# Feed-forward input product of a two-layer trunk: three-pass float32 matmuls against one level of Strassen's recursion, with the weights in a ring of half slots

## The chip, the cores and the metric

The kernel runs on one core of one Trainium2 chip. Its engines are TensorE (PE in the profile, its weight loads are PEld), VectorE (DVE), ScalarE (ACT), GpSimd (POOL) and SyncE (SP), which here only issues loads. Time is device microseconds of one execution, without the host. The kernel before takes 1506.7 us, the median of 3 runs (1506.57 to 1506.76).

## The reference, cut to what matters

The trunk has two layers, over 512 tokens of width 1024. Layer 0 mixes tokens by attention, layer 1 by retention; behind each mixer stands a gated feed-forward block, then a gated embedding. The change is in the feed-forward block's first product.

```
D_MODEL, SEQ, DEPTH, FFN_DIM, CONV_WIDTH = 1024, 512, 2, 2816, 3

def conv_gated_ffn(h, w_in, conv_w, conv_b, w_out):
    s = h.shape[1]
    a = h @ w_in                                    # 512 x 1024 by 1024 x 5632
    gate, up = a[..., :FFN_DIM], a[..., FFN_DIM:]
    gpad = jnp.pad(gate, ((0, 0), (CONV_WIDTH - 1, 0), (0, 0)))
    conv = conv_b + sum(gpad[:, tap:tap + s] * conv_w[tap] for tap in range(CONV_WIDTH))
    return (jax.nn.silu(conv) * up) @ w_out

def reference(x, ...):
    for i in range(DEPTH):
        ...                                         # x = x + mixer
        x = x + conv_gated_ffn(rmsnorm(x, norm_ffn[i]), ffn_w_in[i], ffn_conv_w[i], ffn_conv_b[i], ffn_w_out[i])
        x = per_layer_embed(x, p[i], norm_pl[i], pl_w_gate[i], pl_w_proj[i])
    return rmsnorm(x, norm_final)
```

## The kernel before

Everything is held transposed: 128 features on the partitions, the 512 tokens along the free axis. A product of 128 output features with K input features is K/128 blocks of weights, each 128x128. Float32 is kept by splitting every operand into a high part (rounded to the format fp32r) and a low part (the rest), and by three matmuls for each block (`three`): high by high, high by low, low by high.

Weights come as tiles of 8 blocks (1024 columns, 512 KB) or, for the second product, 11 blocks. SyncE loads a tile into one of two `raw` buffers; ScalarE writes its high part into `wh` (`tile_high`, L1708); GpSimd subtracts, in pieces of 256 columns, and writes the low part into `wl` (`split_low`, L548); TensorE uses both. `wh` and `wl` are rings of four slots.

The feed-forward block has 22 pairs of chunks. A pair f is 128 gate features and the 128 up features that belong to them. In `ffn_in` TensorE makes the gate chunk (8 blocks, 24 matmuls of 512 columns) and then the up chunk, each in a PSUM bank of its own; four banks go round. VectorE takes a gate chunk (L1346, times the norm's 1/rms `rstd`), applies the three taps (L1348, L1352 twice), takes the up chunk (L1355), multiplies (L1358) and makes the low part of the result (L1108); ScalarE gives the silu (L1889) and the high part. The results of all 22 pairs are kept in `yh` and `yl`. After the last pair `ffn_out` makes 8 output chunks, each over 22 blocks, and VectorE adds each to `x`.

Ahead of each feed-forward block stands the mixer's output product, also 8 chunks, which end 5.6 us apart in layer 0 and 2.8 us apart in layer 1. As each chunk ends, VectorE adds it to `x` (L1148), ScalarE writes the high part of the scaled `x` and its square, and VectorE makes the low part (L1128) and adds the square (L1122): this is `x_phase`. The feed-forward product works on `x` before the division by the rms, so it need not wait for the norm: two matmuls (L626, L627) sum the squares over the partitions after the first chunk, and ScalarE turns them into `rstd` by Ln and Exp (L1740, L1742), with a load of an activation table ahead of them and one behind.

Nothing is scheduled by a planner: each engine's instructions stand in the order in which the source gives them, and each engine works through its own in that order. A wait holds back all that stands behind it on its engine.

## Time and profile before

| what | us |
|---|---|
| median of 3 runs | 1506.7 |
| span of the profiled execution, first to last instruction | 1505.3 |
| TensorE busy | 1491.1 |
| VectorE, ScalarE, GpSimd busy | 849.0, 676.1, 795.6 |
| first product of the block, layer 0 (278.3 to 518.3) | 240.0 |
| second product, layer 0 (518.3 to 638.0) | 119.7 |
| first product, layer 1 (1077.7 to 1317.9) | 240.2 |

The profile lists no other time for the execution than its span. The median lies 1.4 us above it, which is what a run has outside its first and last instruction. Starts are in us from the span's start. A matmul's duration includes its way through the array and overlaps the next one, so the pace of matmuls is read from the distance between starts. A row with "x4" is four instructions of one kind in a row, with the time from the first one's start to the last one's end. The granted TensorE clock is 1.00 of full speed through all the stretches of the table.

### The profile page before, as it was taken

How to read it: one execution, taken by the hardware profiler on the slowest of the kernel's cores; microseconds unless marked ns; L12 is line 12 of the kernel's file. 1: busy time of each engine (PE TensorE's matmuls, PEld its weight loads, DVE VectorE, ACT ScalarE, POOL GpSimd, SP SyncE). 2: the span in 40 equal slices, each digit the busy share in tenths (PEclk: the TensorE clock that was granted, in tenths of full speed). 3: DMA queues.
4: the chain of work that ended last, by engine and by line, in shares of the span. 5: the costliest groups of instructions: out<-in, count | busy, mean ns of one | idle time of the engine just before them, and what ended most of it. 6: DMA issues, size and time to landing. Idle time of an engine off the chain costs nothing.

```text
span 1505.3 us, 19989 instructions
## 1 busy us (share of the span) xinstructions
PE 1491.1 (99%) x6808; PEld 1234.9 (82%) x6808; DVE 849.0 (56%) x1294; ACT 676.1 (45%) x1019; POOL 795.6 (53%) x980
## 2 busy tenths in 40 slices
PE   9999999999999999999999999999999999999997
PEld 6888888888888888888888888888788888888886
DVE  7998996455555411159874655646755555511145
ACT  6887886433323322237563543635633333322243
POOL 5343344666666755457345253551566666655452
PEclk9999999999999999999999999999999999999999
DMA  4121111322222322242132322320222222332221
GB/s 178 57 71 56 42 56 63 106 98 98 98 98 98 133 103 97 73 168 99 56 143 102 107 89 85 133 99 33 94 104 91 98 97 98 118 111 97 93 80 60
DMA packets 42838, 142.14 MB, mean 94 GB/s; under 512 B 4256, under 2 KB 10528, under 8 KB 42784
## 3 DMA queue, kind: packets, MB, share of 16 engines
q1 hardware_dynamic: 41248, 138.82, 26.3%
q10 hardware_dynamic: 1536, 2.61, 0.5%
q8 instruction: 32, 0.52, 0.1%
q14 instruction: 22, 0.18, 0.0%
HBM read 139.32 MB, written 2.10 MB: 94 GB/s over the span
## 4 chain that ended last, share of the span: by engine, by line
PE 96%; DVE 2%; ACT 1%; DMA 1%; issue 0%; POOL 0%; SPq 0%; POOLq 0%; DVEq 0%; ACTq 0%
PE bank L602 26%; PE bank L605 26%; PE bank L606 26%; PE bank L880 3%; PE bank L885 3%; PE bank L884 3%; PE bank L680 2%; PE bank L660 1%; PE bank L661 1%; PE bank L691 1%; PE bank L690 1%; DMA x<-in_xT 1%; PE bank L1033 0%; DVE sumsq L1122 0%; PE bank L663 0%
## 5 line engine op out<-in xcount | busy, mean ns | idle before, releaser
L548 POOL TENSOR_TENSOR wl<-raw,wh 128x256 fp32r<-128x256 f32 x752 | 616.1, 852 | 476.4 <-ACT wh L1708 476.4
L602 PE MATMUL bank<-xh,wh 128*128 128x512 f32 (+1 forms) x1160 | 451.4, 389 | 1.0 <-DVE xl L1128 0.8
L606 PE MATMUL bank<-xh,wl 128*128 128x512 f32 (+1 forms) x1160 | 450.2, 388 | 0.0
L1708 ACT ACTIVATE wh<-raw 128x1024 fp32r<-128x1024 f32 (+1 forms) x212 | 235.0, 1108 | 478.8 <-PE bank L602 388.7
L605 PE MATMUL bank<-xl,wh 128*128 128x512 f32 (+1 forms) x1160 | 450.0, 388 | 0.0
L602 PEld LDWEIGHTS bank<-xh,wh 128*128 128x128 f32 x1160 | 217.8, 188 | 47.2 <-DVE xl L1128 2.1
L606 PEld LDWEIGHTS bank<-xh,wl 128*128 128x128 f32 x1160 | 217.9, 188 | 44.7
L605 PEld LDWEIGHTS bank<-xl,wh 128*128 128x128 f32 x1160 | 217.8, 188 | 43.8
L564 POOL TENSOR_TENSOR wl<-raw,wh 128x256 fp32r<-128x256 f32 x160 | 127.2, 827 | 194.4 <-ACT wh L1708 194.4
L1148 DVE TENSOR_TENSOR x<-x,bank 128x512 f32<-128x512 f32 x56 | 38.5, 688 | 254.0 <-PE bank L606 254.0
L602 PE MATMUL bank<-yh,wh 128*128 128x512 f32 x352 | 136.9, 389 | 0.0
L605 PE MATMUL bank<-yl,wh 128*128 128x512 f32 x352 | 136.9, 389 | 0.0
L606 PE MATMUL bank<-yh,wl 128*128 128x512 f32 x352 | 136.9, 389 | 0.0
L1352 DVE SCALAR_TENSOR_TENSOR conv<-gate,par,conv 128x512 f32<-128x512 f32 x88 | 91.8, 1043 | 13.2 <-DVE conv L1348 5.0
L1346 DVE TENSOR_TENSOR gate<-bank,rstd 128x512 f32<-128x512 f32 x44 | 30.4, 692 | 91.8 <-PE bank L606 87.0
L606 PEld LDWEIGHTS bank<-yh,wl 128*128 128x128 f32 x352 | 66.1, 188 | 13.8
L602 PEld LDWEIGHTS bank<-yh,wh 128*128 128x128 f32 x352 | 66.1, 188 | 13.8
L605 PEld LDWEIGHTS bank<-yl,wh 128*128 128x128 f32 x352 | 66.1, 188 | 13.5
L1889 ACT ACTIVATE conv<-conv 128x512 f32<-128x512 f32 x44 | 27.9, 634 | 105.8 <-DVE conv L1352 105.8
L1355 DVE TENSOR_TENSOR up<-bank,rstd 128x512 f32<-128x512 f32 x44 | 30.4, 692 | 68.1 <-PE bank L606 68.1
L1108 DVE TENSOR_TENSOR yl<-yf,yh 128x512 f32 x44 | 41.6, 946 | 40.1 <-ACT yh L1708 40.1
L880 PE MATMUL bank<-wh,sums_h 128*128 128x512 f32 x128 | 50.8, 397 | 0.2 <-ACT sg L1968 0.2
(224 smaller groups left out, 2332.4 us busy)
## 6 DMA issues: line engine op xcount, KB each, us to landing
raw<-in_w SPq DMA_DIRECT2D x180, 512.0 KB, 3.2
raw<-in_w SPq DMA_DIRECT2D x32, 704.0 KB, 4.0
rc<-in_w SPq DMA_DIRECT2D x16, 512.0 KB, 3.8
w_end<-in_w SPq DMA_DIRECT2D x8, 512.0 KB, 4.1
rb<-in_w SPq DMA_DIRECT2D x8, 512.0 KB, 5.9
x<-in_xT SPq DMA_DIRECT2D x4, 512.0 KB, 7.5
pin<-in_pT ACTq DMA_DIRECT2D x2, 512.0 KB, 3.1
rotary<-in_consts ACTq DMA_DIRECT2D x1, 512.0 KB, 3.5
```

Source lines behind the costliest of these rows:

```text
L548: last = nc.gpsimd.tensor_tensor(wl[:, slot, cols], part[:, cols], wh[:, slot, cols].bitcast(F32), ALU.subtract)
L564: last = nc.gpsimd.tensor_tensor(wl[:, slot_of(n), cols], part[:, cols] if len(part.shape) == 2 else part[:, b, :], wh[:, slot_of(n), cols ...
L602: first = mm(out, ah_, bh_, start=start, stop=False, skip_group_check=True)
L605: mm(out, ah_, bl_, start=False, stop=False, skip_group_check=True)
L606: return mm(out, al_, bh_, start=False, stop=stop, skip_group_check=True)
L880: first = mm(out[:], high, wh[:, slot, cols], start=start and k == 0, stop=False, skip_group_check=True)
L884: mm(out[:], high, wl[:, slot, cols], start=False, stop=False, skip_group_check=True)
L885: last = mm(out[:], low_, wh[:, slot, cols], start=False, stop=k == KC // 2 - 1, skip_group_check=True)
L1108: vec.tensor_tensor(out, full, high.bitcast(F32), ALU.subtract).then_inc(done, 1)
L1148: vec.tensor_tensor(one(x, k), one(x, k), bank[u][:], ALU.add).then_inc(chunk_freed, 1)
L1352: vec.scalar_tensor_tensor(cv, g[:, tap:tap + T], col(par, w[tap]), cv, ALU.mult, ALU.add).then_inc(conv_step, 1)
L1708: nc.scalar.activation(out, in_, ACT.Copy, bias=0.0, scale=scale).then_inc(done, 1)
```

## The change

Let A be the weights of a pair, X the input; the K axis is cut in halves, the tokens are cut in an early and a late half of 256, and the two chunks of a pair (gate and up) are the halves of the output. Each is then a 2x2 block problem, and one level of Strassen's recursion (in Winograd's form) gives it by 7 half-size products instead of 8:

* 7 products for each pair, each 4 blocks and 12 matmuls of 256 columns, of these weights: A11, A12, A22 as they are, and S1, S2, S3, S4, which are sums. VectorE makes the sums for each pair: S1 and S3 by one instruction of 1024 elements (`sums_31`, out of `raw` with A21 broadcast), S2 and S4 by one of 512 each.
* The input's sums T1 to T4 (half the K axis by half the tokens) are made once in each layer, together with their high and low parts, at the end of `x_phase` and behind it.
* The weights' ring has 11 half slots of 512 columns. Each of the 7 pieces gets a high part by ScalarE (`piece_high`, 512 columns) and a low part: GpSimd makes six (two instructions of 256 columns each, `piece_lows`), VectorE the one of S4.
* A pair is loaded at once, 1024 KB, into one of two halves of `raw`. The half is free for the next but one load when S4 is summed and GpSimd has made the low part of A22.
* Three products of a pair pile up in one bank: ScalarE copies it (256 columns) after each of A11, S2 and S3 ("snapshots"), before TensorE may add the next. VectorE adds the snapshots to the other banks: `late_up`, `gate_sum`; `late_up_scaled`, `early_up`, `gate_scaled` multiply by `rstd`. The convolution's last tap goes to ScalarE (`tap`), the other two stay on VectorE and work in PSUM.
* The pairs are done in two phases of 11. After each phase the 8 output chunks are made over the 11 blocks of the phase and added to `x`, so `yh` and `yl` hold 11 pairs.

TensorE's order in the middle of a phase is, in the function `ffn`: A11 of pair f, A22 of f-1, S1 of f, S4 of f-1, S2 of f, A12 of f, S3 of f. The diff, cut to its core:

```diff
+HS = K2 * P
+RING_HS = 11
+PHASES = 2
+def ffn_order():
+    order = []
+    for ph in range(PHASES):
+        a, b, last = ph * FH, ph * FH + 1, ph * FH + FH - 1
+        order += [("A11", a), ("S1", a), ("A12", a), ("A11", b), ("S1", b), ("A12", b), ("S2", a), ("S2", b),
+                  ("S3", a), ("S3", b), ("A22", a), ("S4", a)]
+        for f in range(a + 2, last + 1):
+            order += [("A11", f), ("A22", f - 1), ("S1", f), ("S4", f - 1), ("S2", f), ("A12", f), ("S3", f)]
+        ...
+ON_VECTOR = ("S4",)
...
@@ SyncE: a load of a pair waits for the pair before the last
+                def consumed(item):
+                    kind, t = item
+                    if kind == "P":
+                        sp_eng.wait_ge(f_sum4, pair_no(layer, t) + 1)
+                        sp_eng.wait_ge(f_low_p, low_count(layer, PIECE["A22", t]))
...
@@ GpSimd
+            def piece_lows(layer):
+                for q, (kind, _) in enumerate(PIECES):
+                    if kind in ON_VECTOR:
+                        continue
+                    part, at = piece_source(q), piece_at(layer, q)
+                    blocks_ = FH if kind == "O" else K2
+                    pool.wait_ge(f_high, piece_count(layer, q))
+                    for b in range(0, blocks_, LOW_BLOCKS):
+                        ...
+                        last = nc.gpsimd.tensor_tensor(wl[:, held], part[:, cols], wh[:, held].bitcast(F32),
+                                                       ALU.subtract)
+                    last.then_inc(f_low_p, 1)
...
@@ TensorE
-            def ffn_in(layer, norm):
-                ...
-                        x_blocks(slot_of(n0 + u), bank[u][:], range(KC), norm if first and u == 0 else None)\
-                            .then_inc(chunk_done, 1)
-                        if first and u == 0:
-                            stats(norm)
+                def product(kind, f, out, start, stop):
+                    q = PIECE[kind, f]
+                    low_ready(q)
+                    for k in range(K2):
+                        last = three(out, *weights(q, k), *operands[kind](k), start and k == 0, stop and k == K2 - 1,
+                                     begins=k == 0, begun=f_begun)
+                    last.then_inc(f_prod, 1)
+                ...
+                def p2(f, ph):
+                    if f == 0:
+                        pe.wait_ge(x_low, KC * norm + KC)
+                ...
+                def p6(f):
+                    pe.wait_ge(f_snap1, pair_no(layer, f) + 1)
+                    ...
+                    product("S2", f, pair_banks(f)[0], False, False)
+                def p7(f):
+                    pe.wait_ge(f_snap2, pair_no(layer, f) + 1)
+                    ...
+                    product("S3", f, pair_banks(f)[0], False, False)
+                def p4(f):
+                    pe.wait_ge(f_snap3, pair_no(layer, f) + 1)
+                    ...
+                    product("A22", f, pair_banks(f)[0], False, True)
+                ...
+                    for f in range(a + 2, end + 1):
+                        p1(f, ph)
+                        p4(f - 1)
+                        p5(f, ph)
+                        p3(f - 1)
+                        p6(f)
+                        p2(f, ph)
+                        p7(f)
...
@@ VectorE
+            def sums_31(layer, f):
+                ...
+                dve.wait_ge(f_loaded[region], count)
+                others = raw_blocks(("P", f)).rearrange("p (a c) -> p a c", c=HS)[:, 0:4:3, :]
+                vec.tensor_tensor(s31[:, f % 2, :, :], others,
+                                  quarter(f, "A21").unsqueeze(1).to_broadcast([P, 2, HS]), ALU.add).then_inc(f_sum31, 1)
...
@@ ScalarE
+            def snapshot(layer, f, kind, j, done):
+                act.wait_ge(f_prod, product_count(layer, kind, f))
+                copy(snap[:, f % 2, j, :], pair_banks(f)[0], done)
```

How the instructions stand on the engines shows at three places. The first is VectorE in the middle of the first product. Before, one pair is (from its gate chunk on; `ISA` and `REGISTER_ALU` rows are the sequencer's):

```order
L1346 TENSOR_TENSOR gate<-bank,rstd 128x512 [waits chunk_done]
L1348 ISA [waits chunk_freed]
L1348 TENSOR_SCALAR conv<-gate,par 128x512
...
L1352 SCALAR_TENSOR_TENSOR conv<-gate,par,conv 128x512
...
L1352 SCALAR_TENSOR_TENSOR conv<-gate,par,conv 128x512
...
L1355 TENSOR_TENSOR up<-bank,rstd 128x512 [waits chunk_done]
...
L1358 TENSOR_TENSOR yf<-conv,up 128x512 [waits gate_silu]
L1108 ISA [waits y_high]
L1108 TENSOR_TENSOR yl<-yf,yh 128x512
```

Now one turn of the loop is these 13, of which `s<-` are the sums for the pair after the next, `wl<-s,wh` is S4's low part, and `wide_bank` is PSUM:

```order
L1714 TENSOR_TENSOR up<-wide_bank,snap 128x256 [waits f_snap3]
L1718 SCALAR_TENSOR_TENSOR up<-up,rstd 128x256 [waits f_up2]
L1751 TENSOR_TENSOR wide_bank<-wide_bank,up 128x512 [waits gate_silu,f_up1,f_up]
L1510 TENSOR_TENSOR s<-raw 128x1024 [waits f_loaded1,f_low_p]
L1377 TENSOR_TENSOR yl<-wide_bank,yh 128x512 [waits y_high]
L1724 SCALAR_TENSOR_TENSOR up<-wide_bank,rstd 128x256 [waits f_prod]
L1518 TENSOR_TENSOR s<-s,raw 128x512 [waits f_sum31,f_sum4,f_low_p]
L1377 TENSOR_TENSOR wl<-s,wh 128x512 [waits f_high]
L1732 TENSOR_TENSOR wide_bank<-wide_bank,snap 128x2x256 [waits f_prod]
L1736 TENSOR_TENSOR gate<-wide_bank,rstd 128x512 [waits f_gsum]
L1524 TENSOR_TENSOR s<-s,raw 128x512 [waits f_sum2,f_low_v]
L1742 SCALAR_TENSOR_TENSOR wide_bank<-gate,par,wide_bank 128x512 [waits conv_tap]
```

The thirteenth is a second row of L1742's kind (L1744). Seven instructions for a pair have become thirteen, five of which read two operands in SBUF: L1718, L1510, L1518, the second L1377 and L1524.

The second place is ScalarE in the same loop, one turn, from the third snapshot of pair f-1 on:

```order
L2148 ACTIVATE snap<-wide_bank 128x256 [waits f_prod]
L2148 ACTIVATE wh<-raw 128x512 [waits f_loaded0,f_begun]
L2431 ACTIVATE wide_bank<-wide_bank 128x512 [waits conv_step]
L2148 ACTIVATE snap<-wide_bank 128x256 [waits f_prod,f_gsum]
L2148 ACTIVATE wh<-raw 128x512 [waits f_loaded1,f_begun]
L2148 ACTIVATE yh<-wide_bank 128x512 [waits y_full]
L2148 ACTIVATE wh<-s 128x512 [waits f_sum31,f_begun]
L2148 ACTIVATE wh<-s 128x512 [waits f_sum4,f_begun]
L2148 ACTIVATE wh<-s 128x512 [waits f_sum2,f_begun]
L2148 ACTIVATE snap<-wide_bank 128x256 [waits f_prod]
L2426 ACTIVATE wide_bank<-gate,par 128x512 [waits y_low,f_gate]
L2148 ACTIVATE wh<-raw 128x512 [waits f_loaded0,f_begun]
```

One more `wh<-s` (S3) ends the turn. The second row is A11 of pair f+1, the first to need that pair's load; silu, the snapshots and the high part of y stand behind it. Before, a turn was two casts of 1024 columns, one silu and one high part.

The third place is ScalarE at the start of the block, behind the last chunk of `x_phase` (`t`, `xg` and `th` hold the input's sums):

```order
L2148 ACTIVATE th<-t 128x1024 [waits t2_made]
L2148 ACTIVATE wh<-s 128x512 [waits f_sum31,f_begun]
L2148 ACTIVATE th<-xg 128x1024 [waits t3_made]
L2148 ACTIVATE snap<-wide_bank 128x256 [waits f_prod]
L2148 ACTIVATE wh<-raw 128x512 [waits f_loaded0,f_begun]
L2148 ACTIVATE th<-t 128x1024 [waits t4_made]
L2447 ACT_TABLE_LOAD
L2148 ACTIVATE wh<-s 128x512 [waits f_sum4,f_begun]
L2148 ACTIVATE snap<-wide_bank 128x256 [waits f_prod] x3
L2230 ACTIVATE ln_ms<-wide_bank,eps 128x512 [waits stat_done]
L2232 ACTIVATE rstd<-ln_ms 128x512 [waits ms_ln]
L2463 ACT_TABLE_LOAD
```

Before, only the table loads, Ln and Exp stood there. Now the first snapshot stands behind the high part of T3, and the next three behind that of T4.

## Rows read from the trace of the kernel before

**Rows 1.** Page, part 1: busy us of each engine, share of the span, instructions.
```profile
PE 1491.1 (99%) x6808; PEld 1234.9 (82%) x6808; DVE 849.0 (56%) x1294; ACT 676.1 (45%) x1019; POOL 795.6 (53%) x980
```
**Rows 2.** Busy time by stretch: length, PE, PEld, DVE, ACT, POOL, TensorE clock.
```profile
278.30:518.30 240.00, 240.00 (x1060) 198.49 (x1059) 127.26 (x159) 79.90 (x93) 157.01 (x181) 1.00 0.28 100
```
**Rows 3.** Timeline of TensorE, embedding's last chunk: start, us, operation.
```profile
1479.84 0.39 PE L602 MATMUL bank<-xh,wh 128*128 128x512 f32 x1
...
1487.09 0.39 PE L606 MATMUL bank<-xh,wl 128*128 128x512 f32 x1
1487.32 0.28 PE L602 MATMUL bank<-xh,wh 128*128 128x256 f32 x1
...
1492.95 0.28 PE L606 MATMUL bank<-xh,wl 128*128 128x256 f32 x1
```
**Rows 4.** Timeline of GpSimd and VectorE, three tiles' low parts.
```profile
652.20 2.83 POOL L548 TENSOR_TENSOR wl<-raw,wh 128x256 fp32r<-128x256 f32 x4 [4.24 <-ACT wh L1708]
...
481.85 3.74 POOL L548 TENSOR_TENSOR wl<-raw,wh 128x256 fp32r<-128x256 f32 x4 [2.24 <-ACT wh L1708]
481.99 1.15 DVE L1352 SCALAR_TENSOR_TENSOR conv<-gate,par,conv 128x512 f32<-128x512 f32 x1 [0.15 <-DVE conv L1348]
483.29 0.99 DVE L1352 SCALAR_TENSOR_TENSOR conv<-gate,par,conv 128x512 f32<-128x512 f32 x1 [0.15 <-DVE conv L1352]
...
487.20 3.28 POOL L548 TENSOR_TENSOR wl<-raw,wh 128x256 fp32r<-128x256 f32 x4 [1.61 <-ACT wh L1708]
488.26 0.93 DVE L1108 TENSOR_TENSOR yl<-yf,yh 128x512 f32 x1 [0.92 <-ACT yh L1708]
```
**Rows 5.** The same in retention, with a VectorE instruction of 1024 elements.
```profile
918.88 2.42 POOL L564 TENSOR_TENSOR wl<-raw,wh 128x256 fp32r<-128x256 f32 x2
919.22 1.49 DVE L1440 TENSOR_TENSOR w_end<-rc,w_end 128x1024 f32<-128x1024 f32 x1
```
**Rows 6.** Groups of VectorE, whole span: count, busy us, mean ns, idle before.
```profile
L1108 DVE TENSOR_TENSOR al<-sp,ah 128x256 fp32r<-128x256 f32 x16 | 6.7, 419 | 2.3 <-ACT ah L1708 2.2
L1108 DVE TENSOR_TENSOR wl<-ahead,wh 128x1024 fp32r<-128x1024 f32 x2 | 2.4, 1212 | 0.0
```
**Rows 7.** Groups of ScalarE, whole span.
```profile
L1708 ACT ACTIVATE pinh<-pin 128x512 fp32r<-128x512 f32 x4 | 2.3, 624 | 8.8 <-DMA pin<-in_pT 8.8
L1829 ACT ACTIVATE sp<-bank 128x256 f32<-128x256 f32 x16 | 6.1, 382 | 1.1
L1708 ACT ACTIVATE sums_h<-sums 128x1024 fp32r<-128x1024 f32 x4 | 4.2, 1052 | 0.0
L2042 ACT ACT_TABLE_LOAD x4 | 5.1, 1283 | 0.1
```
**Rows 8.** Loads: count, KB each, median us from issue to landing.
```profile
raw<-in_w SPq DMA_DIRECT2D x180, 512.0 KB, 3.2
raw<-in_w SPq DMA_DIRECT2D x32, 704.0 KB, 4.0
```
**Rows 9.** Timeline of VectorE and ScalarE at the first product's start, layer 0.
```profile
272.87 0.69 DVE L1148 TENSOR_TENSOR x<-x,bank 128x512 f32<-128x512 f32 x1 [3.48 <-PE bank L606]
...
278.47 0.69 DVE L1148 TENSOR_TENSOR x<-x,bank 128x512 f32<-128x512 f32 x1 [3.65 <-PE bank L606]
279.08 0.75 DVE L1128 SCALAR_TENSOR_TENSOR xl<-x,par,xh 128x512 fp32r<-128x512 f32 x1
279.74 0.68 DVE L1122 TENSOR_TENSOR sumsq<-sumsq,bank 128x512 f32<-128x512 f32 x1
...
284.51 0.69 ACT L1740 ACTIVATE ln_ms<-bank,eps 128x512 f32<-128x512 f32 x1 [1.76 <-PE bank L627]
285.23 0.63 ACT L1742 ACTIVATE rstd<-ln_ms 128x512 f32<-128x512 f32 x1
```
**Rows 10.** Timeline of VectorE there in layer 1: the last two chunks.
```profile
1075.09 0.69 DVE L1148 TENSOR_TENSOR x<-x,bank 128x512 f32<-128x512 f32 x1 [0.85 <-PE bank L606]
...
1077.89 0.69 DVE L1148 TENSOR_TENSOR x<-x,bank 128x512 f32<-128x512 f32 x1 [0.26 <-PE bank L606]
```

More of the change, by code:

```diff
@@ L58 @@
 FFN_IN_TILES, FFN_OUT_TILES = 2 * FC, 2 * KC
+K2 = KC // 2
 PL_TILES = KC * PC // W8 + KC
@@ new lines, with done_by, ffn_ring @@
+OUT_AT = (6, 0, 3, 6, 0, 3, 8, 5)
+def done_by(q):
+    kind, t = PIECES[q]
+    if kind == "O" and t % KC < 2:
+        return PIECE["O", t - t % KC + 2]
+    return q + 1
+def ffn_ring(layer):
+    at, free, held, p = [], [], {}, RING_FROM[layer]
+    for q, (kind, t) in enumerate(PIECES):
+        p = OUT_AT[t % KC] if kind == "O" else (p + (q in RING_SKIPS[layer])) % RING_HS
+        slots = range(p, p + (3 if kind == "O" else 1))
+        at.append(p)
+        free.append(max(done_by(held[i]) + 1 if i in held else 0 for i in slots))
+        assert free[-1] <= q and slots[-1] < RING_HS
+        held.update((i, q) for i in slots)
+        p = slots[-1] + 1
+    return at, free, held
@@ L131, with item_load @@
+def item_load(layer, item):
+    i = ITEM[item]
+    return i % 2, 16 * (layer * len(ITEMS) // 2 + i // 2 + 1)
 C_COS, C_SIN, C_DECAY = 0, T, 2 * T
@@ new lines, in x_phase @@
+                    if k == K2 + 3:
+                        sum_2(layer, 1)
+                t2(2)
+                t2(3)
+                x_low_part(norm, KC - 1)
+                add_square(norm, KC - 1, (KC - 1) % 2)
+                sum_high(norm)
+                negative_lows(1, 1)
+                sum_low(norm)
+                for k in range(K2):
+                    t3(k)
+                t3_lows()
+                for k in range(K2):
+                    t4(k)
+                negative_lows(2, 3)
@@ L1471, in tile_low @@
                 dve.wait_ge(w_high, casts(n))
-                low(pieces(wl[:, slot_of(n), cols], part), part, pieces(wh[:, slot_of(n), cols], part), done)
+                held = slot_cols(slot_of(n), cols)
+                low(pieces(wl[:, held], part), part, pieces(wh[:, held], part), done)
             def rotate_first(h, which):
@@ L1719, in tile_high @@
                     act.wait_ge(ready, count)
-                    copy(pieces(wh[:, slot, 0:W8 * P], part), part, w_high)
+                    copy(pieces(wh[:, slot_cols(slot, slice(0, W8 * P))], part), part, w_high)
                     return
+                for layer in range(2):
+                    if N_PL[layer] <= like < N_PL[layer] + RING:
+                        ffn_left(layer, slot)
+                        free = 0
                 if free:
```

736 lines of the change are left out of this document (561 added, 175 removed).

## Prediction, written before the changed kernel was run

> **What bounds the kernel now.** I read the page's busy times first: TensorE works 1491.1 of 1505.3 us and no other engine over 56% [rows 1]. So time falls only where TensorE gets less to do or its pace changes, and an engine beside it matters once it is slower than TensorE for the same work. The stretch of the changed product shows the room: of 240.0 us GpSimd is busy 157.0, VectorE 127.3, ScalarE 79.9, at a full granted clock [rows 2]. For one of the 22 pairs that is 10.9 us of TensorE with 7.1 of GpSimd and 5.8 of VectorE beside it. Then I read the pace of matmuls from their starts, where embedding's last chunk goes from full to half size. 512 columns: 33 steps from 1479.84 to 1487.32, 0.2267 us each. 256 columns: 47 steps from 1487.32 to 1492.95, 0.120 each [rows 3]. Last I read what GpSimd and VectorE do to each other [rows 4, 5], because the change loads just these two.
>
> **TensorE's part.** A pair was 48 matmuls x 0.2267 = 10.88 us and becomes 84 x 0.120 = 10.08: 0.80 us less, 44 pairs, **-35.2 us**. That is the whole gain; an eighth less arithmetic would be 1.36 us a pair, but a half-size matmul takes 53% of a full one.
>
> The Trainium skill (TensorE: Matmul & The Clock Gate, Back-to-back issue gap) gives a warm gap of N/2.4 + 2.5 ns. By it a pair would go from 10.36 to 9.17 us and the gain would be 52 us. The rows have 48 half-size matmuls in a row at 0.120, so they decide.
>
> The second product keeps its 3 x 11 x 16 matmuls; cut in two halves it costs VectorE 8 more additions of 0.69 us in each layer, beside chunks of 7.5 us: nothing.
>
> **GpSimd's part.** Four instructions of 256 columns alone take 2.83 us, one is 0.74 long, so they start 0.70 apart [rows 4]. With one VectorE instruction of 512 elements that reads two operands in SBUF the four take 3.28, with two 3.74: +0.45 each. With one of 1024 elements, two take 2.42 instead of 0.70 + 0.74 = 1.44: +0.98 [rows 5]. The new turn asks 6 pieces x 2 = 12 instructions, 8.4 us, and VectorE has five such instructions in it: three of 512 (1.34), one of 1024 (0.98), one of 256 (no row; between 0 and 0.45, I take 0.18: half of the step from 512 to 1024, 0.27, below the 0.45). Sum **10.9 us a pair**, against 10.08 of TensorE. Before it was 3.74 + 3.28 = 7.0 against 10.9.
>
> **VectorE's part.** One turn is three instructions of 256 (0.42 each), nine of 512 (0.69) and one of 1024 (1.21): 8.7 us [rows 6, 9]. Neighbours overlap by 0.08 (0.69 long, 0.61 from start to start, rows 9), nine times: -0.7. Three wait for the one before them, 0.15 each [rows 4]: +0.45. The five with two SBUF operands wait for GpSimd's instruction to end: 0.93, 0.99 and 1.15 instead of 0.69 [rows 4], +0.24 to +0.46 each, so +1.2 to +2.3. Together 9.7 to 10.8, I take 10.1: level with TensorE. It is a ring with ScalarE: third snapshot, VectorE down to `gate_scaled` (7.7), tap, two casts, next snapshot (0.63 + 2 x 0.62 + 0.38 with 0.1 for each hand-over), also some 10.1 us, and each turn TensorE's A22 waits for that snapshot. ScalarE alone has 7 casts x 0.62, 3 x 0.38 and three of 0.62: 7.3 us [rows 7], room enough.
>
> **Can a lead hide GpSimd's 10.9?** It could if GpSimd could start a phase far ahead. It can't for long: the load of pair f+2 waits for the low part of A22 of pair f. 512 KB land after 3.2 us and 704 after 4.0 [rows 8]; going on at that slope, 1024 KB take 5.3. Behind the load stands ScalarE's cast of A11 of f+2, and behind that silu, the next snapshot and, through silu, VectorE's whole turn. By the durations above GpSimd ends A22 some 3.8 us after it starts A11, so ScalarE's next A11 is free 9.1 us after GpSimd's last A11 began; ScalarE is there after 10.1. Each turn GpSimd falls 0.8 behind; within one or two turns the load comes later than ScalarE, and from there every turn lasts what GpSimd's lasts. 9 of the 11 pairs of a phase stand in this loop, 36 in all: 36 x (10.86 - 10.08) = **+28 us**, less some 3 for the first turns: **+25**.
>
> **The start of each block.** Count from VectorE's addition of the last chunk (278.47 in layer 0; TensorE goes on at 278.27) [rows 9]. Before, the first product wanted the last low part of `x` after 7/8 of 5.4 us. Now A12, third in line, wants it after 2.9. VectorE has six instructions up to it (two of 0.75, four shorter): ready at 4.0. Then come the squares, the high and low parts of T2 and of the squares, four T3 of 0.34, with GpSimd's port delays: 9.7. ScalarE's high part of T3 (1.05), VectorE's low part (1.21), four T4 (1.4), ScalarE's high part of T4 (1.05), a table load (1.28), the cast of S4 (0.62) and only then the snapshot (0.38) that the second pair's S2 waits for: 17.2 with hand-overs [rows 7]. TensorE has seven products before it, 10.1 us, and stands there 7.4 us. Ln, Exp and a table load (0.69 + 0.63 + 1.28) ahead of the first S3 snapshot cost 0.5 more. Last, in the first turn of the loop ScalarE's third snapshot stands behind the tap, which needs S4's product, two VectorE instructions and itself: 4.1 us after that product, where TensorE has one product of 1.44 to do: 2.7. Together **+10.6** in layer 0. In layer 1 chunks end 2.8 us apart instead of 5.6 [rows 10], while VectorE now has some 15 us of work from the fifth chunk on in 8.4 us; it comes 3.2 later: **+13.8**. The second phase of each block has only the last of these stalls, its casts done beside the second product: 2 x 2.7 = **+5.4**. Without port delays the first two would be 8 and 11; if DMA landings or the bank waits come late, some 4 more each.
>
> **Sum.** -35.2 + 25 + 10.6 + 13.8 + 5.4 = +19.6 us. The sum is against the profiled span, 1505.3, which becomes 1525; the 1.4 us around it stay, so the forecast is **1526 us** against the median of 1506.7.
>
> **Rivals.**
> *TensorE's pace holds (GpSimd is not the bound).* If five VectorE instructions don't all meet a busy GpSimd, its turn is nearer 8.4 + 1.2 = 9.6 and VectorE's 9.7. Then loops run at 10.1 and the 25 becomes 1: 1502; with starts at their lower bound, 1494. For it: in this stretch before, VectorE's instructions met GpSimd by their place in the turn, and other places may miss it. Against it: a GpSimd busy for over 9 of 10 us leaves no place to miss. Chance 0.18.
> *The two engines hold each other up more than summed.* Each VectorE instruction waits 0.46 and GpSimd idles for casts that ScalarE has late in its turn (A12 and S3 stand last): 11.5 us a turn, 36 x 0.64 = 23 more than forecast: 1549. For it: three rings lie within 0.8 us of each other, and what one loses another rarely gives back. Chance 0.12.
> *The port is held for a whole instruction.* Then five instructions, 0.42 + 1.21 + 3 x 0.69 = 3.7 us, go fully on GpSimd's 8.4: 12.1 a pair, 1526 + 36 x 1.2 = 1569. Against it: +0.45 for 0.69 in three places [rows 4]. Chance 0.02. [...]
> *The starts overlap far better than I chain them*, half of the 30 us, with the loop as forecast: 1511. Inside the forecast's own range.
>
> **Chances.** The forecast with its own range (1508 to 1540) has 0.68. Within 0.2% (3 us, about what this kernel's runs can tell from no change, 1503.7 to 1509.7) lies the upper edge of the first rival and the lower edge of the forecast: 0.08. Faster by more: most of the first rival, 0.16. Slower by more: 0.76. The range for 8 in 10 takes in the first rival's upper half and the second rival: 1497 to 1549.
>
> **What would show it.** In the changed kernel's profile: matmuls of 256 columns 0.120 apart inside a product, and a turn of the loop (A11 of one pair to A11 of the next) of 10.9 instead of 10.1 us; TensorE idle ahead of A22's first matmul, put down to ScalarE's snapshot; GpSimd busy 9 tenths or more through a phase, its instructions at 0.74 and 1.19 us; 5 us loads that ScalarE's A11 cast waits for. At the start of each block one idle of some 7 us ahead of the second S2 and one of 2 to 3 ahead of the first A22 in the loop. A loop at 10.1 us proves the GpSimd step wrong; 11 us with GpSimd idle for a fifth of it proves the bound to be a ring of waits and not its work; a granted clock below 1.00 in the phases would be a cost I have at nothing.

## The result, and the profile after

| | before | after |
|---|---|---|
| median, us | 1506.7 | 1587.9 (1586.2 to 1590.3, 4 runs) |
| ratio | | 1.054 (95% interval 1.0525 to 1.0555) |
| profiled span, us | 1505.3 | 1587.0 |
| two feed-forward blocks, first matmul to first of embedding, us | 359.7 + 359.9 | 395.6 + 404.8 |

The change costs 81 us and the forecast was 1526 (1497 to 1549): right in sign, 62 us short. All of the 81 us lies in the two blocks. The page of the changed kernel, part 1, beside [rows 1]:

```profile
PE 1491.6 (94%) x8392; PEld 1304.4 (82%) x8392; DVE 1062.5 (67%) x1614; ACT 832.2 (52%) x1431; POOL 974.5 (61%) x1156
```
TensorE is idle for 95 us instead of 14, and as busy as before although its matmuls are 35 us less: some of them now run at half the clock (below). Its waits over the span (us in total, times, longest us):

```profile
PE wide_bank L770 <- ACT snap L2148: 43.4, 44, 5.1
PE wide_bank L770 <- POOL wl L719: 14.0, 4, 3.5
PE wide_bank L770 <- DVE xl L1397: 11.5, 4, 8.4
PE wide_bank L770 <- DVE up L1714: 7.9, 2, 4.1
PE wide_bank L770 <- POOL wl L704: 5.1, 2, 4.5
```
The first and third rows I had forecast. The second, fourth and fifth I had not: the second is ahead of the second chunk of the second product in all four phases, the fourth at the start of the two second phases, the fifth once at the start of embedding in layer 1. Busy time by stretch (length, PE, PEld, DVE, ACT, POOL, granted clock), beside [rows 2]: the first phase of layer 0, the second product behind it, the first phase of layer 1, and 68 us inside the loop:

```profile
277.60:411.60 134.00, 116.23 (x904) 113.04 (x903) 109.63 (x150) 76.32 (x140) 114.71 (x128) 0.95 0.23 77
411.60:479.70 68.10, 64.61 (x289) 53.47 (x289) 16.16 (x23) 16.79 (x20) 33.71 (x49) 0.97 0.31 106
1113.10:1253.10 140.00, 117.33 (x904) 114.25 (x903) 115.58 (x156) 78.85 (x145) 121.91 (x135) 0.94 0.22 74
...
334.00:402.00 68.00, 63.78 (x520) 62.50 (x519) 58.31 (x79) 41.10 (x81) 66.95 (x75) 1.00 0.30 103
```
In the loop GpSimd is busy 66.95 of 68.00. The timeline of TensorE there: A11's first matmuls of three pairs in a row, and the waits between the first two (start, us, operation, idle before and releaser):

```profile
334.36 0.28 PE L770 MATMUL wide_bank<-xh,wh 128*128 128x256 f32 x1
...
337.24 0.28 PE L770 MATMUL wide_bank<-xh,wh 128*128 128x256 f32 x1
337.36 0.28 PE L773 MATMUL wide_bank<-xl,wh 128*128 128x256 f32 x1
...
341.56 0.28 PE L770 MATMUL wide_bank<-xh,wh 128*128 128x256 f32 x1
...
344.28 0.39 PE L770 MATMUL wide_bank<-th,wh 128*128 128x256 f32 x1 [1.12 <-ACT snap L2148]
...
345.82 0.28 PE L770 MATMUL wide_bank<-xh,wh 128*128 128x256 f32 x1
...
356.64 0.28 PE L770 MATMUL wide_bank<-xh,wh 128*128 128x256 f32 x1
```
Half-size matmuls start 0.120 apart, as in [rows 3], and two turns last 11.46 and 10.82. I laid the two blocks out by such starts of products. A stretch's excess over the pace is its length less its matmuls at 0.120 and 0.2267. A phase's loop is counted here from the A11 of its fourth pair to the first matmul of the second product, which is 8 turns; what lies ahead of that A11 is the start:

| | forecast | measured, us |
|---|---|---|
| pace, 44 pairs | -35.2 | -35.2 |
| loop, turns of 10.86 forecast, 10.98 measured (mean of 32) | +25 | +28.8 |
| start of each phase, up to the fourth pair's A11, over the pace | +29.8 | +61.8 (18.5, 8.8, 25.0, 9.5) |
| second product, four stretches over 62.8 | 0 | +26.6 (5.4, 6.5, 3.8, 11.0) |

The sum, +82, is the 81 us within the 1 us of statistics matmuls that stand in the starts. Two rows of the forecast held and two did not.

### The profile page after: what moved, and what is told of

It is laid out like the page before. It is cut to its first block, busy times and chain, and to the rows that moved or that the text cites. A ratio compares the mean times of both kernels' runs of the same rounds, so it can differ in the third digit from the quotient of the medians.

```text
span 1587.0 us, 23224 instructions
## 1 busy us (share of the span) xinstructions
PE 1491.6 (94%) x8392; PEld 1304.4 (82%) x8392; DVE 1062.5 (67%) x1614; ACT 832.2 (52%) x1431; POOL 974.5 (61%) x1156
## 4 chain that ended last, share of the span: by engine, by line
PE 63%; POOL 16%; DVE 8%; DMA 6%; ACT 4%; issue 3%; SPq 0%; DVEq 0%; ACTq 0%; POOLq 0%
PE wide_bank L770 16%; PE wide_bank L774 16%; PE wide_bank L773 16%; POOL wl L719 15%; DMA raw<-in_w 5%; PE wide_bank L1151 3%; PE wide_bank L1156 3%; PE wide_bank L1155 3%; PE wide_bank L849 2%; ACT wh L2148 2%; DVE s L1510 2%; DVE wl L1377 1%; DVE s L1518 1%; DVE gate L1736 1%; DVE wide_bank L1732 1%
## 5 line engine op out<-in xcount | busy, mean ns | idle before, releaser
L2148 ACT ACTIVATE wh<-raw 128x512 fp32r<-128x512 f32 (+2 forms) x264 | 230.8, 877 | 341.8 <-PE wide_bank L770 130.5
L770 PE MATMUL wide_bank<-xh,wh 128*128 128x256 f32 (+1 forms) x1160 | 380.6, 328 | 20.4 <-DVE xl L1397 11.5
L773 PE MATMUL wide_bank<-xl,wh 128*128 128x256 f32 (+1 forms) x1160 | 378.3, 326 | 0.0
L774 PE MATMUL wide_bank<-xh,wl 128*128 128x256 f32 (+1 forms) x1160 | 378.2, 326 | 0.0
L770 PEld LDWEIGHTS wide_bank<-xh,wh 128*128 128x128 f32 x1160 | 224.2, 193 | 40.0 <-DVE xl L1397 13.2
L719 POOL TENSOR_TENSOR wl<-s,wh 128x256 fp32r<-128x256 f32 x264 | 237.9, 927 | 6.4 <-ACT wh L2148 6.4
L774 PEld LDWEIGHTS wide_bank<-xh,wl 128*128 128x128 f32 x1160 | 223.8, 193 | 17.6
L773 PEld LDWEIGHTS wide_bank<-xl,wh 128*128 128x128 f32 x1160 | 224.2, 193 | 16.3
L770 PE MATMUL wide_bank<-th,wh 128*128 128x256 f32 x528 | 158.1, 299 | 43.4 <-ACT snap L2148 43.4
L774 PE MATMUL wide_bank<-th,wl 128*128 128x256 f32 x528 | 152.7, 289 | 0.0
```

What stands on the lines that cost most here:

```text
L719: last = nc.gpsimd.tensor_tensor(wl[:, held], part[:, cols], wh[:, held].bitcast(F32), ALU.subtract)
L770: first = mm(out, ah_, bh_, start=start, stop=False, skip_group_check=True)
L773: mm(out, ah_, bl_, start=False, stop=False, skip_group_check=True)
L774: return mm(out, al_, bh_, start=False, stop=stop, skip_group_check=True)
L2148: nc.scalar.activation(out, in_, ACT.Copy, bias=0.0, scale=scale).then_inc(done, 1)
```

## Experiments

All times are medians; "before" ran beside each at 1506.8 to 1506.9. e4, e6 and e12 ran once, the others four times. A turn is the mean of the 32 turns from the fourth pair's A11 of each phase on, "starts" the third row of the table above.

| kernel | us | ratio to before (95%) | turn | starts |
|---|---|---|---|---|
| after | 1587.9 | 1.054 (1.0525 to 1.0555) | 10.98 | 61.8 |
| e1 O1's cast first | 1566.0 | 1.0391 (1.0374 to 1.0409) | 10.88 | 62.5 |
| e2 ScalarE's start order | 1580.2 | 1.0489 (1.0472 to 1.0507) | 10.91 | 54.9 |
| e4 two lows less | 1563.7 (one run) | | 10.16 | 61.1 |
| e5 filled waits | 1585.8 | 1.052 (1.0503 to 1.0538) | 11.00 | 58.5 |
| e6 = e1 + up2 in PSUM | 1561.5 (one run) | | 10.78 | 60.6 |
| e7 = e6 + S2's low shared | 1557.3 | 1.033 (1.0312 to 1.0349) | 10.67 | 62.2 |
| e8 = e1 + up2 first | 1568.5 | 1.0413 (1.0394 to 1.0432) | 10.88 | 64.8 |
| e9 = e8 + start orders | 1558.7 | 1.0347 (1.0328 to 1.0365) | 10.89 | 53.9 |
| e10 = e7 + casts first | 1541.2 | 1.0229 (1.0212 to 1.0246) | 10.25 | 58.3 |
| e11 = e10 + start orders | 1535.1 | 1.0187 (1.017 to 1.0204) | 10.27 | 51.2 |
| e12 = e11, parts of T3 and T4 left out | 1535.5 (one run) | | 10.34 | 48.8 |
| e13 = e11 + snapshots first | 1535.5 | 1.0192 (1.0175 to 1.0209) | 10.27 | 51.7 |

### e1: the second product's wait

```diff
+                        if f == end + 1:
+                            high("O", KC * ph + 1)
                         if f <= end + 1:
                             tap(f - 1)
...
-                        if f > end:
+                        if f > end + 1:
```


> One edit: ScalarE's cast of the second output slot's weights (O1) stands ahead of the last pair's tap instead of behind it. Theory (order in ScalarE's queue): in the changed kernel TensorE waits 3.5 us four times ahead of the second chunk of the second product, because that cast (1.37) and GpSimd's six lows (3.9) start only after the tap, at 419.55 in the first phase, while the weights' transfer should have landed some 4 us earlier. With the edit the wait goes in all four phases: 14 us, and with it some of the 7.6 us that these stretches lose at a granted clock of 0.5: 1566 to 1574 us. Rival (the slot or the transfer is late, not the cast): the cast starts at the same time as before, and the time stays at 1587 to 1589.

ScalarE, GpSimd and TensorE of the changed kernel there:

```profile
413.70 0.60 ACT L2148 ACTIVATE yh<-wide_bank 128x512 fp32r<-128x512 f32 x1 [1.07 <-DVE wide_bank L1751]
418.83 0.78 ACT L2426 ACTIVATE wide_bank<-gate,par 128x512 f32<-128x512 f32 x1 [4.54 <-DVE gate L1736]
419.55 1.37 ACT L2148 ACTIVATE wh<-raw 128x1408 fp32r<-128x1408 f32 x1
...
421.00 4.58 POOL L719 TENSOR_TENSOR wl<-raw,wh 128x256 fp32r<-128x256 f32 x7 [9.77 <-ACT wh L2148]
...
424.93 0.63 PE L770 MATMUL wide_bank<-yh,wh 128*128 128x512 f32 x1 [3.49 <-POOL wl L719]
```
and ScalarE in e1:

```profile
413.77 1.38 ACT L2148 ACTIVATE wh<-raw 128x1408 fp32r<-128x1408 f32 x1 [1.06 <-DMA raw<-in_w]
417.26 0.78 ACT L2426 ACTIVATE wide_bank<-gate,par 128x512 f32<-128x512 f32 x1 [2.10 <-DVE gate L1736]
```
ScalarE and GpSimd stood idle for 4.5 and 9.8 us with the cast queued behind a tap that needs the last S4 product. In e1 the cast waits for the transfer alone, the wait is gone in all four phases, three of the four second products last 62.8 us, and the kernel gains 21.9. That is the theory: 14.0 of waits and, with them, the time at half clock, 7.6 us in the expectation and 6.9 by the stretches below. The fourth second product keeps 4.7 us, from another wait (see "Why the prediction was wrong").

### e4, e6, e7, e10: what bounds the loop

e4: GpSimd's loop over a piece ends after the first half where `kind in ('A12', 'S3')`, from the fourth pair on.

> From the fourth pair of each phase on GpSimd makes only the first half of the low parts of A12 and S3; the second halves are left out (the product uses old values there), nothing else is changed. A turn of the loop has 10 GpSimd instructions instead of 12. Theory (GpSimd's own work is the bound of the loop): 10.98 us a turn less 2 x 0.70 is 9.6, below TensorE's 10.08, so turns fall to TensorE's pace or to VectorE's ring, 10.1 to 10.3, in 28 turns: 19 to 25 us less, 1563 to 1569, and GpSimd shows idle time. Rival (the ring of snapshots, VectorE's turn and the tap holds the loop at 10.98): turns stay over 10.7 with GpSimd idle for over 1 us in each, and the time stays over 1580.

e6 (here f_up2's sum; the multiplication that follows reads the same bank):

```diff
-vec.tensor_tensor(up2[:, f % 2, :], pair_banks(f)[2], ...
+vec.tensor_tensor(bank[6 + f % 2][:, 0:HALF], pair_banks(f)[2], ...
```


> On top of e1 (1566.0 us, loop turns of 10.9): VectorE's sum up2 goes to a free PSUM bank instead of SBUF, so the 256-element multiplication by rstd that follows reads one operand in SBUF instead of two. VectorE's work stays, and one of its five instructions that hold GpSimd up goes. Theory (GpSimd's turn is its 8.4 us plus the holds, and I had no row for this one: 0.18 taken between 0 and 0.45): turns fall by 0.1 to 0.25, 36 turns, 4 to 9 us: 1557 to 1562. Rival (a short instruction holds up nothing): turns and time stay within 0.05 us and 2 us.

e7:

```diff
+            def half_low(layer, f):
+                ...
+                low(wl[:, at:at + HS // 2], s2[:, HS // 2:HS], wh[:, at:at + HS // 2], f_low_x)
...
                         if f < end:
+                            half_low(layer, f + 1)
                             sum_4(layer, f + 1)
```


> On top of e6: from the third pair of each phase on VectorE makes the second half (256 elements) of the low part of S2, so GpSimd has 11 instructions a turn instead of 12 and VectorE one of 0.42 more, which again reads two operands in SBUF. Theory (GpSimd's turn is a sum): less 0.70, plus a hold of 0.1 to 0.25 as in e6, so turns of 10.3 to 10.5 instead of e6's 10.75; 36 x 0.45 is 16 us less than e6: 1542 to 1547. Rival (VectorE's ring is the next bound right away, since it is 0.86 busy and gets work): turns stay over 10.6, gain under 6 us, and GpSimd shows over 0.3 us of idle time a turn.

e10:

```diff
-                        if f <= end + 1:
-                            tap(f - 1)
                         if f < end:
                             high("A12", f + 1)
                             high("S3", f + 1)
+                        if f <= end + 1:
+                            tap(f - 1)
```


> On top of e7 (1557.3 us, turns of 10.67 with GpSimd idle for a tenth): ScalarE casts A12 and S3 of the next pair ahead of the tap instead of behind it. Theory (with GpSimd's share smaller the loop is bound by the ring third snapshot, VectorE down to the gate, tap, two casts, next snapshot, the one that the prediction had at 10.1): the two casts, 1.24 us, leave the ring, turns fall to 10.1 to 10.35, 32 turns: 10 to 18 us less, 1540 to 1547. Rival (VectorE's own work with its waits for GpSimd's port is the bound, no ring): turns stay over 10.6 and the gain is under 3 us.

Busy time in 34 us of the loop for e6, e7 and e10 in this order, and in 68 us for e4 (one fence for each):

```profile
364.00:398.00 34.00, 32.64 (x268) 32.03 (x267) 29.19 (x42) 21.09 (x41) 34.00 (x38) 1.00 0.33 111
```
```profile
364.00:398.00 34.00, 31.15 (x253) 30.34 (x252) 31.48 (x46) 21.18 (x41) 29.93 (x34) 1.00 0.26 93
```
```profile
364.00:398.00 34.00, 34.00 (x280) 33.49 (x280) 33.65 (x48) 22.80 (x42) 34.00 (x38) 1.00 0.29 103
```
```profile
334.00:402.00 68.00, 68.00 (x569) 68.00 (x568) 63.02 (x88) 45.58 (x89) 64.61 (x70) 1.00 0.26 90
```
e4 decides the first question. With two GpSimd instructions less seven of the eight turns of each phase are 10.08, TensorE's pace, and GpSimd still works 64.61 of 68: 9.58 a turn, which is 10.98 less twice 0.70. So in the changed kernel GpSimd's own work is the bound, and the ring of snapshots, with its casts where they were, lets 10.08 through. The turns gave 26.1 us and the kernel's one run is 24.2 below the median; the changed kernel's own four runs differ by 4.

e6 prices the hold that I had no row for: the settled turns in the first phase of layer 0 are 10.96 to 10.99 in e1 and 10.78 to 10.80 in e6, **0.18 us** for an instruction of 0.42, the value I took. The other phases are less even, and over all 32 turns the mean falls by 0.10. The Trainium skill (SBUF — State Buffer, Who interferes with whom) calls the shared port an exclusive lock and says that a VectorE instruction with two SBUF inputs contends with a GpSimd one that reads SBUF. The runs agree on who interferes; the price is less than half of the instruction.

e7 is the miss that taught most. GpSimd lost an instruction and was idle (29.93 of 34 us busy), yet turns fell only to 10.67, 3.6 us over 32 of them (the kernels' times differ by 4.2, and e7's own runs by 4.5). That is the rival's number: a ring of waits. The trace's chain of work in e7 shows which one (start, us, what):

```profile
368.03 0.62 ACT wh L2168
368.72 7.52 POOL wl L728 x8
376.30 4.92 DMA raw<-in_w
381.84 0.59 ACT wide_bank L2451
388.18 0.70 DVE gate L1755
389.63 1.14 ACT wh L2168 x2
```
The cast of A12, eight low parts up to A22's, the load that waits for these, silu (behind the A11 cast that waits for the load), VectorE's work down to the gate, the tap, and the cast of A12 again: 21.6 us for two turns, 10.8 for one. This ring goes through the load and not from snapshot to snapshot as the forecast's. e10 cuts it: the casts of A12 and S3 no longer wait for the tap. Turns are 10.27 to 10.30 with few exceptions, GpSimd and VectorE are both busy for 33.65 us and more of 34, and the kernel gains 16.1 (theory: 10 to 18). The theory's time came true, but its ring isn't shown: taking the two casts out of a ring of snapshots would help as well, and e4 had passed that ring at 10.08 with the casts in it. e10 ran only on top of e7. What its order is worth with all twelve instructions on GpSimd, which are 10.98 a turn by themselves, was not tested.

### e2, e9, e11, e12, e13: the start of a block

e2 moves snapshots, Ln, Exp and table loads ahead on ScalarE:

```diff
                 piece_high(layer, 9)
+                snap1(layer, 0)
+                snap1(layer, 1)
+                nc.scalar.preload_act_table_set("natural_log_exp_and_others")
                 t3_highs(layer)
-                snap1(layer, 0)
+                snap2(layer, 0)
                 piece_high(layer, 10)
+                snap2(layer, 1)
+                norm_scale(norm, FFN_STAT)
+                nc.scalar.preload_act_table(ACT.Silu)
                 t4_highs(layer)
-                nc.scalar.preload_act_table_set("natural_log_exp_and_others")
...
```


> One edit, ScalarE's order at the start of a block: the snapshots of the first two A11 products stand ahead of the high part of T3, those of the two S2 products, Ln, Exp and both table loads ahead of the high part of T4. Theory (snapshots are queued behind work that waits for VectorE): the two waits ahead of the S2 products (2.4 and 3.9 in layer 0, 0.9 and 5.1 in layer 1) go, about 2 us come back ahead of A22, which needs T4, so A22 of the first pair starts some 7 us earlier in each layer; with the clock that falls in these waits 12 to 20 us in all: 1568 to 1576. Rival (VectorE and GpSimd set the start whatever ScalarE's order is): the second pair's A22 waits as much longer as the S2 waits shrink, and the time stays within 4 us of 1588.

e9 has this, e8, and on VectorE:

```diff
                     if k == K2 + 1:
                         t1_lows()
                         sum_2(layer, 0)
-                        sums_31(layer, 1)
                     if k == K2 + 2:
                         t2(0)
                         t2(1)
-                        sum_4(layer, 0)
-                    if k == K2 + 3:
-                        sum_2(layer, 1)
+                x_low_part(norm, KC - 1)
+                sums_31(layer, 1)
                 t2(2)
                 t2(3)
-                x_low_part(norm, KC - 1)
                 add_square(norm, KC - 1, (KC - 1) % 2)
+                sum_4(layer, 0)
+                negative_lows(1, 1)
+                sum_2(layer, 1)
                 sum_high(norm)
-                negative_lows(1, 1)
...
```


> On top of e8: ScalarE's start order of e2, and VectorE's at the start of a block: the low part of the last chunk of x directly behind its addition, the sums S3 and S1 of the second pair, S4 of the first and S2 of the second behind it instead of ahead of it (ScalarE's casts follow). Theory (the waits at the start are VectorE's queue: in layer 1 it does 5.6 us of sums ahead of the last chunk's low part, and TensorE waits 8.4 us for that): the wait ahead of the first A12 falls to under 1.5 in layer 0 and to 2 to 4 in layer 1, and the first A22 starts 8 to 12 us earlier than in e1 in layer 0 and 10 to 14 in layer 1: 1535 to 1548. Rival (VectorE's sum of work in the start is the bound, wherever the sums stand): the wait ahead of A12 goes but A22 starts no more than 7 us earlier, as with ScalarE's order alone: 1550 to 1556.

> On top of e10: the orders of VectorE and ScalarE at the start of a block from e9, without e8's edit. Theory (the loops and the starts are separate costs, so gains add): e9 took 8.6 us off the starts of e1 (62.5 to 53.9 over the pace of 10.08); the same comes off e10: 1531 to 1540, still slower than before's 1506.9. Rival (the earlier start only moves the wait into the first turns of the loop, where GpSimd has not got ahead): less than 3 us off e10.

VectorE of the changed kernel in layer 1 around the last addition of a chunk, and the TensorE wait behind it, answering [rows 10]:

```profile
1111.41 1.22 DVE L1518 TENSOR_TENSOR s<-s,raw 128x512 f32<-128x512 f32 x1
1112.56 1.75 DVE L1510 TENSOR_TENSOR s<-raw 128x1024 f32<-128x1024 f32 x1
1114.24 0.68 DVE L1417 TENSOR_TENSOR x<-x,wide_bank 128x512 f32<-128x512 f32 x1
...
1118.50 1.21 DVE L1524 TENSOR_TENSOR s<-s,raw 128x512 f32<-128x512 f32 x1
1119.63 0.67 DVE L1417 TENSOR_TENSOR x<-x,wide_bank 128x512 f32<-128x512 f32 x1
...
1125.03 0.58 PE L770 MATMUL wide_bank<-xh,wh 128*128 128x256 f32 x1 [8.36 <-DVE xl L1397]
```
The last chunk's addition comes 6.5 us after TensorE went on (1113.1), not 3.2 as I had it, in part since sums of 0.69 and 1.21 take 1.2 and 1.75 beside a busy GpSimd. e9 takes the wait to 3.4 in layer 1 and to nothing in layer 0, as its theory had it. But the first A22, counted from the block's first matmul, comes only 4.5 and 7.1 us earlier than in e1, the rival's bound, and the kernel takes 1558.7, 9.8 less than e8, 7.4 less than e1, and over both expected ranges (1535 to 1548, the rival's 1550 to 1556). ScalarE's order alone (e2) gave 7.7, where its theory had 12 to 20 and its rival at most 4: A22 came 6.2 us earlier in layer 0, and 5.6 in layer 1, but it now waits 2.25 itself in both, the S4 behind it 1.2 and 1.9, and the second pair's A22 still 1.1 and 3.2 (2.9 and 3.4 in the changed kernel). In e11 the start orders give 6.1 without e8, inside the theory's time.

> On top of e11, VectorE makes one of the four instructions for T3 and one of the four for T4 and leaves out the other six (the products that use T3 and T4 then take partly old values); everything else is issued as before. Theory (the start of a block is VectorE's work end to end, with its waits for GpSimd): six instructions of 0.47 to 0.96 us less on its chain, so the first A22 of each block starts 3 to 5 us earlier and the time falls by 6 to 10 us. Rival (ScalarE's queue or the transfers of the next weights set it): under 2 us a block.

> On top of e11 (1535.1 us, computed in full): at the start of a block ScalarE takes the snapshots of the first two A11 products before the casts of S2, S3 and S3 (it waited for VectorE's S2 sum, which waits for GpSimd), and VectorE splits the sum of squares before it makes that S2 sum. Theory (the start is a chain through all three engines, GpSimd's low of S2, VectorE's S2 sum, ScalarE's casts, GpSimd's lows): the wait ahead of the first S2 goes (2.6 us in layer 0, 2.4 in layer 1), but the second S2 and the first A22 hang on the same chain, so A22 starts only about 1 us earlier in each block: 1531 to 1535. Rival (the snapshot is what holds the start, as ScalarE's order in e2 suggested): A22 starts 2.5 us earlier or more in each block: 1528 to 1531.

Both came out as no gain (1535.5 and 1535.5 against 1535.1). In e12 the starts are 2.4 us shorter and the loops 2.2 longer; the first A22 comes no earlier. ScalarE there shows why:

```profile
295.75 0.38 ACT L2165 ACTIVATE snap<-wide_bank 128x256 f32<-128x256 f32 x1 [1.24 <-PE wide_bank L783]
296.21 0.69 ACT L2247 ACTIVATE ln_ms<-wide_bank,eps 128x512 f32<-128x512 f32 x1
296.93 0.63 ACT L2249 ACTIVATE rstd<-ln_ms 128x512 f32<-128x512 f32 x1
297.58 1.28 ACT L2467 ACT_TABLE_LOAD   x1
298.87 1.06 ACT L2165 ACTIVATE th<-t 128x1024 fp32r<-128x1024 f32 x1
```
VectorE had T4 ready at 296.1, but its high part stands behind Ln, Exp and the table load, as my e2 ordered them: the rival of e12. In e13 the first S2 starts 2.2 us earlier in layer 0 and the first A22 at 300.64 instead of 300.72; counted from the block's first matmul it is 0.3 earlier in layer 1. Which order is the shortest for this start stays open: each of the three tried met the next queue.

### e8: the start of the second phase

```diff
-                        if f == a + 1:
-                            sums_31(layer, f + 1)
                         if f <= end + 1:
                             late_up(f - 1)
                             late_up_scaled(f - 1)
+                        if f == a + 1:
+                            sums_31(layer, f + 1)
```


> On top of e1: at the start of each phase VectorE makes the sum up2 of the first pair before it waits for the weights of the third pair (sums S3 and S1), not behind that wait. Theory (VectorE's queue order holds TensorE: at the start of the second phase it stands 7.2 us waiting for a transfer of 4.9 us with up2 queued behind, and TensorE waits 4.0 for up2): the wait ahead of the first S4 goes, but the third pair's A11 needs the same transfer, so some 2 us of it come back there; 2 to 4 us less in each second phase, 0 to 2 in each first: 1557 to 1562. Rival (all of it comes back at the third pair's A11, since the transfer is the bound): the time stays within 2 us of 1566.

The first row is what VectorE waits for between 470 and 500 us in the changed kernel, the second fence is e8's chain of work and TensorE's row:

```profile
DVE s L1510 <- DMA raw<-in_w: 8.7, 2, 7.0
```
```profile
487.47 4.81 DMA raw<-in_w
...
495.50 0.55 PE L770 MATMUL wide_bank<-xh,wh 128*128 128x256 f32 x1 [3.81 <-POOL wl L719]
```
The rival is right that nothing is gained, and the kernel is even 2.4 us slower than e1, just outside its 2 us. In the second phases the wait moves from up2 to the third pair's A11: that pair's 1024 KB can only be asked for when GpSimd has made A22's low part of the phase's first pair, at 487.4, and everything behind it is 4.8 us away. A third place for raw weights would test it directly; that was not tried. The second phases' starts are 0.4 and 0.1 us shorter than in e1, the first phases' 1.5 and 1.4 longer: the loss is there, where the sums of the third pair now stand behind an up2 that waits for its snapshot (in layer 0 they start at 306.6 instead of 303.5).

### e5: what the fallen clock costs

```diff
+                def keep_on(count, at):
+                    for _ in range(count):
+                        mm(bank[at][:, 0:HALF], ones_r[:], xh[:, 0, 0:HALF], start=True, stop=True, ...)
```


> TensorE gets matmuls of 256 columns that nobody reads (into a free bank) where it waits at the start of a block: 16 and 56 ahead of A12 of the first pair (layer 0, layer 1), 14 and 4 ahead of the first S2, 24 and 34 ahead of the second, 16 and 20 ahead of A22 of the second pair, each about two thirds of the wait. No wait is taken away. Theory (the granted clock falls because TensorE stands idle there): the stretches at 0.5 that follow these waits go, and with them most of the 10.5 us that the first phases of the two blocks lose by the clock (4.7 and 5.8): 1576 to 1581 us, granted clock at 1.00 from 290 to 320 and from 1120 to 1170. Rival (the clock falls for another reason, or what follows waits for VectorE anyway): the half-clock stretches stay, or go without the time getting shorter by over 3 us.

The start of the two blocks in the changed kernel, then in e5:

```profile
277.00:330.00 53.00, 39.97 (x282) 38.13 (x281) 40.62 (x56) 27.64 (x48) 35.12 (x39) 0.87 0.17 60
1113.00:1175.00 62.00, 43.97 (x311) 42.61 (x310) 50.07 (x66) 32.05 (x56) 45.12 (x49) 0.86 0.16 52
```
```profile
277.00:330.00 53.00, 46.63 (x371) 44.90 (x371) 40.86 (x57) 28.13 (x49) 38.01 (x42) 1.00 0.17 60
1113.00:1175.00 62.00, 55.41 (x435) 53.63 (x433) 50.11 (x68) 33.81 (x59) 47.05 (x51) 0.97 0.19 67
```
The clock is back and the time falls by only 2.1 us, which is inside the 3 us that the rival allows and within what the changed kernel's runs differ by. The trace says where the rest went. Up to the fourth pair's A11 the two blocks win 2.6 and 2.5 us, over half of the 9 that the stretches at 0.5 had cost there; so a part was hidden behind the other engines' chain and a part was not. The loops behind them then take 0.2 and 0.8 longer, and the second phase of layer 0, which has no filler, starts 1.7 slower in this execution.

## Why the prediction was wrong

**TensorE's part: right.** 0.120 a matmul, -35.2.

**GpSimd's part and "Can a lead hide": right in cause and size.** Turns of 10.98 for 10.86, GpSimd busy 66.95 of 68, loads of 4.9 us for 5.3, and e4's 10.08 with 9.58 of work; the loops cost 28.8 for 25. (The text's own terms, 8.4 + 1.34 + 0.98 + 0.18, give 10.90; it went on with 10.86, 1.4 us less in 36 turns. The first rival's lower end, 1494, is 1497 by the bounds that the text gives for the starts.) The holds of 0.45, 0.98 and 0.18 made the difference to the first rival, and the third rival's whole-instruction price (12.1) is excluded.

**VectorE's ring "some 10.1": not contradicted, but not the next bound.** In e4, with VectorE's and ScalarE's instructions unchanged, turns are 10.08, so the ring takes no more than that there. The text followed the load only as a lag behind GpSimd; what it didn't price is the ring through the load, 10.8 a turn in e7, where VectorE has one instruction more. It cost nothing here, hidden behind GpSimd's 10.98, and it is why taking work off GpSimd alone gave so little.

**"The second product keeps its matmuls ... nothing": the step that failed first.** It counted VectorE's eight more additions and did not follow the new order of casts: O1's cast stands behind a tap that needs the product two before it. 26.6 us for 0; e1 gives back 21.9. The other 4.7 are nearly all a wait of 4.5 for the first tile of embedding in layer 1: its cast waits for TensorE, as I read it for the slot that the last chunk of weights holds. No run changed this:

```profile
1513.40 1.06 ACT L2148 ACTIVATE wh<-raw 128x1024 fp32r<-128x1024 f32 x1 [9.50 <-PE wide_bank L774]
...
1517.87 0.80 PE L770 MATMUL wide_bank<-pinh,wh 128*128 128x512 f32 x1 [4.51 <-POOL wl L704]
```
The text said that such a thing exists ("DMA landings or the bank waits come late, some 4 more each") and put it only at the starts.

**"The start of each block": places right, sizes half.** Layer 0 cost 18.5 for 10.6. The second S2 starts 20.9 us after the block's first matmul, 10.9 over its pace for 7.4: VectorE's chain is longer, with T3's and T4's first two instructions at 0.95 each instead of the 0.47 of their last two. A22 in the first turn waits 2.9 for 2.7. What I left out is the next load, in the chain of work:

```profile
310.01 5.75 DMA raw<-in_w
```
The third pair's 1024 KB are asked for only after the first A22's low part, and from that pair's A11 to the fourth's it takes 15.1 us. Layer 1 cost 25.0 for 13.8, some 3.3 of it since VectorE was 6.5 late and not 3.2.

**The second phases "have only the last of these stalls": wrong.** 8.8 and 9.5 for 2.7. The same load: VectorE waits 7.0 for it with up2 behind (e8). My own sentence on the loop, that a load waits for A22's low part, was not carried to the first turn of a phase, where nothing leads.

**The clock "at nothing": wrong in the row, and in the sum where nothing hides it.** Behind the waits TensorE's clock was granted at 0.5, the 1.2 GHz level. Matmuls of 256 columns then start 0.213 apart:

```profile
299.11 0.21 PE wide_bank L773
299.32 0.21 PE wide_bank L774
299.53 0.21 PE wide_bank L770
```
Added up over all matmuls that start in the stretches that the trace lists at 0.5, less 0.120 or 0.2267 each, it is some 20 us: 9.0 at the block starts, 4.3 in the second phases and 6.9 in the second products. At the block starts filling the waits wins 5.1 up to the fourth pair's A11 and 2.1 in the whole (e5). In the second product, where after O1 TensorE waits for nobody, it goes with the wait in e1. There the clock is 0.57 in the stretch behind the wait:

```profile
425.00:429.00 4.00, 4.00 (x11) 3.13 (x12) 0.00 (x0) 0.00 (x0) 3.73 (x6) 0.57 0.54 180
```

In sum, of the missing 62 us 22 are an order in a queue that I did not follow (shown by e1), nearly 5 a slot at the start of embedding, 4 the loops, and 32 a load and a chain at the starts whose links I had, but not for these places. That last part is read from the traces; the runs on it (e2, e8, e9, e11) each gave back only some of it.

## What to carry to other kernels

Where a kernel's queues are written by hand, follow for each product its last operand back through every queue, to the transfer too, at the ends of the loops above all: the loop's turn was forecast within some 1%, the seams were 59 us off. Before moving work off the busy engine, price the next ring, transfers included: here taking a twelfth of GpSimd's work away gave 4 us (e7), and an order of two casts and a tap on top of it 16 more (e10). The best version, e11, is computed in full and takes 1535.1, 1.9% above before: half-size matmuls at 53% of a full one leave Strassen 35 us, and its seams still take 51.

## What the runs showed of the hardware

- A VectorE instruction of 256 elements with two operands in SBUF costs a busy GpSimd 0.18 us (e6); those of 512 and 1024 cost 0.45 and 0.98 [rows 4, 5]. The other way round VectorE pays too: two-operand instructions of 0.47 take 0.95, of 0.69 up to 1.2 and of 1.21 up to 1.75, when they meet GpSimd's.
- The granted clock was 0.5 behind waits of 1.9 to 8.4 us, but not behind every one: not behind one of 2.8 (at 283.4), one of 1.7, nor the third of the four waits of 3.5 ahead of O1. With the waits of layer 0's start filled it was 1.00 there (e5). At 0.5 half-size matmuls start 0.213 apart instead of 0.120.
- A TensorE wait costs more than its idle time: around the wait of 1.12 shown above two products take 4.26 (341.56 to 345.82) instead of 2.88, 0.26 more than the wait. 0.16 of it is the last matmul's way through the array, which the profile counts as busy (0.28 long, 0.12 from start to start).
